# Hybrid trunk layer on one Trainium2 core: q and u of the input projection by seven half-block products per pair of feature blocks

## The reference

```python
h = rms_norm(x, mix_norm_g[l])
proj = h @ w_in[l]
u_a, v_a, q, k, v = jnp.split(proj, splits, axis=-1)      # 512, 512, 512, 128, 128 columns
y_a = spatial_gating(u_a, v_a, sgu_ln_g[l], sgu_ln_b[l], sgu_w[l], sgu_b[l])
y_b = window_sink_attention(q..., k..., v..., sinks[l], rel_bias)
y_a = rms_norm(y_a, group_norm_g[l, :D_A])
y_b = rms_norm(y_b, group_norm_g[l, D_A:])
x = x + jnp.concatenate([y_a, y_b], axis=-1) @ w_out[l]
h = rms_norm(x, ffn_norm_g[l])
x = x + (jax.nn.silu(h @ w_gate[l]) * (h @ w_up[l])) @ w_down[l]
return rms_norm(x, final_norm_g)
```

## Time and profile before

| what | value |
|---|---|
| median of 3 runs | 931.95 us (931.64 to 932.1) |
| span of the profiled execution | 930.2 us |
| TensorE busy | 921.3 us, 99% of the span |
| VectorE, ScalarE, GpSimd busy | 551.3, 403.6 and 329.1 us |
| mean granted TensorE clock | 0.998 |

### The profile page before, as it was taken

How to read it: one execution, slowest core, us unless ns; L and a number is a source line. 1 busy time by engine, 2 the same in 40 slices (tenths; PEclk the granted TensorE clock), 3 DMA queues, 4 the chain that set the end, 5 groups by cost and what they waited for, 6 DMA issues and landing times.

```text
span 930.2 us, 11930 instructions
## 1 busy us (share of the span) xinstructions
PE 921.3 (99%) x4277; PEld 757.5 (81%) x4277; DVE 551.3 (59%) x812; ACT 403.6 (43%) x833; POOL 329.1 (35%) x344
## 2 busy tenths in 40 slices
PE   9999999999999999999999999999999999999997
PEld 7888888878778878888888888888888888888885
DVE  5655773576677966564553645537446676544753
ACT  6743541465655733333333323333335355434451
POOL 1410000022125288575674765755753100000022
PEclk9999999999999999999999999999999999999999
DMA  9621312312224334726437365273557897656643
GB/s 337 229 79 57 89 41 88 88 46 87 73 98 130 102 114 158 226 77 218 153 108 227 99 195 179 90 241 90 182 179 259 317 394 230 188 198 194 191 138 133
DMA packets 132000, 147.02 MB, mean 158 GB/s; under 512 B 16281, under 2 KB 92645, under 8 KB 131941
## 3 DMA queue, kind: packets, MB, share of 16 engines
q1 hardware_dynamic: 131268, 145.86, 48.3%
q10 hardware_dynamic: 672, 0.40, 0.1%
HBM read 105.73 MB, written 40.50 MB: 157 GB/s over the span
## 4 chain that ended last, share of the span: by engine, by line
PE 94%; issue 2%; DVE 2%; DMA 1%; ACT 0%; POOL 0%; DVEq 0%; POOLq 0%; ACTq 0%
PE ps L703 30%; PE ps L705 29%; PE ps L704 29%; PE ps L830 1%; PE ps L849 1%; PE ps L907 1%; PE ps L840 1%; PE ps L779 1%; DMA A22s<-in_w_gate 1%; DVE P_lo L1703 0%; DMA small<-in_mix_gT 0%; DVE T_lo L1690 0%; PE ps L733 0%; PE ps L736 0%; PE ps L739 0%
## 5 line engine op out<-in xcount | busy, mean ns | idle before, releaser
L1703 DVE TENSOR_TENSOR P_lo<-P_raw,P_hi 128x512 fp32r<-128x512 f32 x132 | 118.1, 910 | 82.5 <-ACT P_hi L1227 75.2
L703 PE MATMUL ps<-T_hi,P_hi 128*128 128x512 f32 x352 | 137.1, 389 | 0.0
L705 PE MATMUL ps<-T_hi,P_lo 128*128 128x512 f32 x352 | 136.9, 389 | 0.0
L704 PE MATMUL ps<-T_lo,P_hi 128*128 128x512 f32 x352 | 136.9, 389 | 0.0
L703 PE MATMUL ps<-rb_hi,ra_hi 128*128 128x512 f32 x308 | 119.8, 389 | 0.0
L704 PE MATMUL ps<-rb_lo,ra_hi 128*128 128x512 f32 x308 | 119.8, 389 | 0.0
L705 PE MATMUL ps<-rb_hi,ra_lo 128*128 128x512 f32 x308 | 119.8, 389 | 0.0
L647 POOL TENSOR_TENSOR wd<-wd 128x256 f32<-128x256 f32 x88 | 82.9, 942 | 95.0 <-DMA wd<-in_w_down 89.9
L1328 ACT ACTIVATE ra_hi<-ra 128x512 fp32r<-128x512 f32 x77 | 48.6, 632 | 98.3 <-DMA rb<-w_down_T 58.1
L1783 DVE TENSOR_TENSOR ra_lo<-ra,ra_hi 128x512 fp32r<-128x512 f32 x77 | 56.2, 730 | 37.6 <-ACT ra_hi L1328 37.3
L1227 ACT ACTIVATE P_hi<-P_raw 128x512 fp32r<-128x512 f32 x132 | 76.6, 620 | 3.5 <-POOL P_raw L607 3.5
(11 more groups left out here) (208 smaller groups left out, 1911.4 us busy)
## 6 DMA issues: line engine op xcount, KB each, us to landing
wd<-in_w_down SPq DMA_DIRECT2D x44, 256.0 KB, 3.3
w_down_T<-wd SPq DMA_DIRECT2D x22, 512.0 KB, 5.0
ra<-act_S SPq DMA_DIRECT2D x44, 256.0 KB, 2.7
rb<-w_down_T SPq DMA_DIRECT2D x44, 256.0 KB, 3.0
act_S<-Q SPq DMA_DIRECT2D x33, 256.0 KB, 3.7
ra<-act_A SPq DMA_DIRECT2D x33, 256.0 KB, 5.0
rb<-in_w_down SPq DMA_DIRECT2D x33, 256.0 KB, 5.9
P_raw<-in_w_gate SPq DMA_DIRECT2D x22, 256.0 KB, 3.7
```

The source lines that it names most:

```text
L703: mm(dst, lhs[0], rhs[0], start=start, stop=False, skip_group_check=onto)
L704: mm(dst, lhs[0], rhs[1], start=False, stop=False, skip_group_check=onto)
L705: return mm(dst, lhs[1], rhs[0], start=False, stop=stop, skip_group_check=onto)
L1703: tt(w_l[p, m][:], src[:], w_h[p, m][:].bitcast(F32), ALU.subtract).then_inc(w_split, 1)
```

## The change

For each of four pairs of feature blocks (q0 with q1, q2 with q3, u0 with u1, u2 with u3) the product of a 1024 x 256 block of w_in with the two halves of the rows is seen as 2x2 blocks times 2x2 blocks, of 512 in k, and done by seven products of 12 (`in_product`) in place of eight of 12. The work goes stage by stage: P1 for the four pairs, then P2, P6, P5, P7, P3 and P4, in banks 0, 1, 2 and 7 for one family (accumulated) and 5 and 6 for the other.

- The combinations of x (D1 to D4) are built from a second load of xT: GpSimd subtracts, ScalarE scales by `mix_g` and makes the hi part, VectorE the lo part. The gain is now in hT, and no longer in the weights.
- The combinations of the weights (s1 = A21 + A22, s2 = s1 - A11, A11 - A21, A12 - s2) are GpSimd sums of freshly loaded blocks.
- Products are taken out by ScalarE (`product_copy`, 12), summed by VectorE (`product_add`, 12) and GpSimd (U + V, 4), and multiplied by `roots` on VectorE (`corner`, 16).
- The spatial blocks now all lie in P1 and P2, and the mixed values go back into `vn`. The gates and square sums go to GpSimd, the value copies to ScalarE. The woA blocks and the woB loads get new places. The totals of the first norm are taken in two halves, with a root each. The gelus of the last three blocks of u come behind the exponentials of row block 0.

```diff
-    ITEMS = ["k", "v", "u0", "u1", "u2", "u3", "A0", "A1", "A2", "q0", "A3", "q1", "q2", "q3"]
-    UNITS = [(c, h) for c in ("k", "v", "u0", "u1", "u2", "u3") for h in range(2)]
-    UNITS += [(f"q{t}", h) for h in range(2) for t in range(G)]
+    ITEMS = ["k", "v"]
+    UNITS = [(c, h) for c in ITEMS for h in range(2)]
+    IN_BANK_A, IN_BANK_B = (0, 1, 2, 7), (5, 6)
+    IN_ORDER = {p: (2, 3, 0, 1) if p == "P4" else (0, 1, 2, 3) for p in PR}
+    GATES = ((0, 1), (2, 1), (1, 0), (3, 0), (0, 0), (2, 0), (1, 1), (3, 1))
+    YA_SUMS = ((1, 0, 2), (2, 3, 4), (2, 0, 5), (2, 3, 6), (1, 0, 7), (1, 3, 8))
...
 GpSimd
+            for k in range(4):
+                pool.wait_ge(d_scaled, D_SCALED["D4"] + k + 1)
+                pool.wait_ge(combo_hi, k + 1)
+                combine(D_raw["D4"][:, k], D_raw["D4"][:, k], D_hi["D2"][:, k].bitcast(F32), ALU.subtract).then_inc(d_summed, 1)
+                pool.wait_ge(combo_ready, k + 1)
+                pool.wait_ge(d_summed, 12 + 2 * k + 1)
+                combine(D_raw["D4"][:, k], D_raw["D4"][:, k], D_lo["D2"][:, k].bitcast(F32), ALU.subtract).then_inc(d_summed, 1)
+            gate(0)
+            for i in range(4):
+                pool.wait_ge(slot_in[i], 4 * BLOCK[i])
+                combine(wA_raw[i][:], stg[i][:], wA_raw[i][:], ALU.subtract).then_inc(w_summed, 1)
+            gate(1)
+            for i in range(4):
+                pool.wait_ge(copied, copied_at("P5", i))
+                combine(U[:, i], U[:, i], V[:, i], ALU.add).then_inc(uv_added, 1)
+                pool.wait_ge(slot_in[4 + i], 2 * BLOCK[i])
+                combine(wB_raw[i][:], wB_raw[i][:], s2[i][:], ALU.subtract).then_inc(w_summed, 1)
+            ya_sum(0)
+            gate(2)
+            gate(3)
+            ya_sum(1)
+            gate(4)
+            ya_sum(2)
+            gate(5)
+            ya_sum(3)
+            gate(6)
+            gate(7)
+            rootA(0)
+            ya_sum(4)
+            ya_sum(5)
...
 TensorE
+            def in_product(p, i):
+                pe.wait_ge(w_split, in_split_at(p, i))
...
+                elif p == "P5":
+                    pe.wait_ge(combo_ready, 8)
+                    if i < 2:
+                        pe.wait_ge(c_summed, added_at("P2", i + 2))
+                    else:
+                        pe.wait_ge(copied, copied_at("P5", i - 2))
...
+                for k in range(4):
+                    last = split_mm(ps[:, in_bank(p, i), :], (hi[:, k], lo[:, k]), (rows[0][:, k], rows[1][:, k]), k == 0 and not onto, k == 3, onto)
+                last.then_inc(prod_done, 1)
...
             def value_windows(w):
-                if w in (0, 3):
+                if w < 2:
                     pe.wait_ge(ya_mixed, 2 * HA)
                 else:
-                    pe.wait_ge(ya_summed, 2 * HA - 2)
+                    pe.wait_ge(vwin_ready, w - 1)
...
-            unit(NQ1)
+            in_product("P3", 0)
+            value_windows(0)
+            value_windows(1)
+            in_product("P3", 1)
+            value_windows(2)
+            value_windows(3)
+            in_product("P3", 2)
             logits(0)
-            unit(NQ1 + 1)
-            unit(NQ1 + 2)
+            in_product("P3", 3)
+            for i in IN_ORDER["P4"][:3]:
+                in_product("P4", i)
             probs_T(0, 0)
-            unit(NQ1 + 3)
+            in_product("P4", IN_ORDER["P4"][3])
             probs_T(0, 1)
             logits(1)
             values(0)
+            ya_totals(0)
...
 ScalarE
+            for i in range(4):
+                in_weight_hi("P5", i)
+                d_scale("D3", i)
+                if i >= 2:
+                    u_gelu(i - 2)
+            for k in range(4):
+                d_scale("D4", k)
...
+            for i in range(4):
+                in_weight_hi("P7", i)
+                product_copy("P5", i)
+                d_to_hi("D4", i)
...
+            ya_hi_rows(0)
+            ya_hi_rows(1)
+            ya_square(0)
+            ya_square(1)
+            u_gelu(2)
+            woA_piece(2)
+            u_gelu(3)
+            woA_piece(3)
+            value_copy(0)
+            value_copy(1)
...
             for _half in probabilities(0):
                 pass
+            u_gelu(5)
+            u_gelu(6)
+            u_gelu(7)
+            ya_hi_rows(4)
+            ya_square(4)
+            ya_hi_rows(5)
+            ya_square(5)
             probs_to_sbuf(0, 0)
+            ya_hi_rows(6)
+            ya_square(6)
+            ya_hi_rows(7)
             probs_to_sbuf(0, 1)
+            ya_square(7)
...
 VectorE
+            for i in range(4):
+                in_weight_lo("P5", i)
+            for k in range(4):
+                d_to_lo("D3", k)
+            for i in range(4):
+                in_weight_lo("P7", i)
+                d_to_lo("D4", i)
+            in_weight_lo("P3", 0)
+            product_add("P7", 0)
+            corner("P7", 0)
+            in_weight_lo("P3", 1)
+            woA_piece(0)
+            product_add("P7", 1)
+            corner("P7", 1)
+            in_weight_lo("P3", 2)
+            woA_piece(1)
+            product_add("P7", 2)
+            corner("P7", 2)
+            in_weight_lo("P3", 3)
+            ya_lo_rows(0)
+            product_add("P7", 3)
+            corner("P7", 3)
```

More of the change, by code:

```diff
@@ L300, in hybrid_trunk_layer @@
         wd_in, wd_summed, wd_out = sem("wd_in"), sem("wd_summed"), sem("wd_out")
-        step_in = [sem(f"step_in{n}") for n in range(NSLOT)]
         y_in, step_hi, step_split, step_done, prod_out, y_added = (
@@ new lines, in product_add, with corner @@
+            def product_add(p, i):
+                dve.wait_ge(prod_done, in_at(p, i))
+                if p == "P2":
+                    dve.wait_ge(copied, copied_at("P1", i))
+                else:
+                    dve.wait_ge(uv_added, i + 1)
+                dst = {"P2": GP, "P7": V, "P3": U}[p]
+                tt(dst[:, i], ps[:, in_bank(p, i), :], dst[:, i], ALU.add).then_inc(c_summed, 1)
+            def corner(p, i):
+                f, half = CORNER[p]
+                if p == "P4":
+                    dve.wait_ge(prod_done, in_at(p, i))
+                    src = ps[:, in_bank(p, i), :]
+                else:
+                    dve.wait_ge(c_summed, added_at(p, i))
+                    src = {"P2": GP, "P7": V, "P3": U}[p][:, i]
+                if i < 2:
+                    if p == "P7" and i == 0:
+                        dve.wait_ge(ya_gated, 2)
+                    chunks = "p (c q) -> p c q"
+                    stt(qT[half][:, :, 2 * i + f, :], src.rearrange(chunks, q=CH), SCALE, roots[half][:].rearrange(chunks, q=CH), ALU.mult, ALU.mult).then_inc(c_out, 1)
+                else:
+                    tt(GATE_U[2 * CORNERS.index(p) + i - 2], src, roots[half][:], ALU.mult).then_inc(c_out, 1)
@@ new lines, in ya_lo_rows, with ya_total_sums @@
+            def ya_lo_rows(g):
+                h, half = GATES[g]
+                rows = slice(HT * half, HT * half + HT)
+                dve.wait_ge(ya_hi_ready, g + 1)
+                tt(ya[:, rows, 1, h, :], vn[:, h, rows], ya[:, rows, 0, h, :].bitcast(F32), ALU.subtract).then_inc(ya_ready, 1)
+            def ya_total_sums(half):
+                dve.wait_ge(ya_total, half + 1)
+                nc.vector.tensor_reduce(ssqA[:, HT * half:HT * half + HT], ps[:, 7, :].rearrange("p (t n) -> p t n", n=P), AX.X, ALU.add).then_inc(ssqA_ready, 1)
@@ L1579, in _ @@
-            evict(NQ0 + 3)
-            evict(NQ1)
+            for i in range(4):
+                in_weight_lo("P2", i)
+            ya_mix(0)
+            ya_mix(1)
+            d_to_lo("D2", 2)
+            d_to_lo("D2", 3)
+            in_weight_lo("P6", 0)
+            ya_mix(2)
+            ya_mix(3)
+            for i in range(4):
+                d_to_lo("D1", i)
+                if i:
+                    in_weight_lo("P6", i)
+                if i == 2:
+                    ya_mix(4)
+                    ya_mix(5)
+                product_add("P2", i)
+                corner("P2", i)
@@ new lines, in _ @@
+            in_weight_lo("P3", 2)
+            woA_piece(1)
+            product_add("P7", 2)
[4 more added lines that the diff above has]
+            corner("P7", 3)
+            woA_piece(2)
+            product_add("P3", 0)
+            corner("P3", 0)
+            ya_lo_rows(1)
+            woA_piece(3)
+            product_add("P3", 1)
+            corner("P3", 1)
+            in_weight_lo("P4", 0)
+            ya_lo_rows(2)
@@ L1582, in add_bias @@
+            product_add("P3", 2)
+            corner("P3", 2)
+            in_weight_lo("P4", 2)
             def add_bias(r):
```

659 lines of the change are left out of this document (423 added, 236 removed).

## The result

The changed kernel takes 943.54 us (median of 4 runs, 942.83 to 944.71) against 931.98 us for the kernel before on the same chip: ratio 1.0126, 95% interval 1.0112 to 1.014. The profiled execution has a span of 941.0 us against 930.2: +10.8. The prediction said +6.4 and 938.4 us, with P3(2) 11 us late and a lower clock in new gaps as a rival of its own. The measured time lies in its whole range (926 to 946 us) and above the range of the forecast's own case (934 to 942).

What follows compares the result with a forecast made beforehand. TensorE, 99% busy, bounds the kernel; GpSimd and VectorE together decide the change. Output projection 5.3 late, plus 0.7 and 0.4, gives +6.4 on the 930.2 us span: 936.6, measured 938.4; whole range 926 to 946, own case 934 to 942.

Steps and rivals of the forecast that it cites:

- P3(2): Third product of P3, input projection: can start at 153.5 us and not 142.4, 11.1 us late, spending the whole gain.
- the forecast's own case: Whole kernel: +6.4 us on the profiled span, 938.4 us measured, own range 934 to 942 us; chance 0.55.
- Removed work: Input projection on TensorE: 384 products become 336, 48 fewer at 0.2267 us each, 10.9 us less.
- P5(2): Third product of P5, due 118.8 us: 0.5 to 4 us late, waiting for ScalarE's copy of P5(0); swallowed by the later wait.
- Transfers, `mix_g`, the items at 0: Input projection: extra loads and issues, the gain moved from wv to xT, and merged k and v operations each cost 0.
- Exclusion: GpSimd additions and VectorE operations with two SBUF inputs run one at a time: 1.74 us a pair, 44.5 us from 105.5.
- Corner(P7,3): VectorE's last corner of P7, needed by the next chain: 150.0 us by the exclusive sum, taken as 150.3 with waits.
- The clock at 0: TensorE's granted clock: the forecast's sum has no term for a fall in the new gaps, so 0 us.
- rival 3: Granted clock falls to half speed in new gaps before P3(2) and in the tail: 943.8 to 946.5 us; chance 0.12.
- The tail: From P3(2) to the output projection: 26.7 us through ScalarE's queue, 5.9 over TensorE's own 20.8; output projection at 180.2.
- the one microsecond of exclusion: Between P3(2) and the output projection: one microsecond of the GpSimd and VectorE lock, raising 25.7 us to 26.7.
- The rival on the other side: GpSimd and VectorE slip into each other's gaps, without the lock: P3(2) starts at 142.9, 926.8 us; chance 0.21.

## Why the prediction was right, and where it wasn't

**Removed work: right.** Up to 118.4 us every product stands within 0.3 us of where the calendar without waits has it, at 0.227 us pitch. The last of the 24 matmuls of P5(0) and (1) starts at 118.40, so the next was possible at 118.6, and P5(2) was due at 118.8.

**Transfers, `mix_g`, the items at 0: right.** No wait of TensorE in the stage is released by a transfer. The one that mattered showed up only in experiments: the woB loads, which I had costed at 0 because `out_unit(0,2)` isn't late. They held ScalarE in front of row block 1's exponentials, 2.8 us, once all ahead of them was faster.

**Exclusion: right, and by the estimate above the largest cost, but the length of GpSimd's own work stands right behind it.** The pair is 1.69 to 1.72 us against 1.74 in the sum. The Trainium skill (SBUF — State Buffer, section "SBUF: two separate sides") has an exclusive lock on the shared port pair, and for a VectorE operation with two SBUF inputs it limits it to GpSimd operations that read SBUF. This case's runs agree: additions hold VectorE's splits to 1.76 us, memsets of nearly the same length, which read nothing, leave them at 0.69, and sums from PSUM stay at 0.68. Corner(P7,3) ended at 150.5 against 150.3. So close a hit is luck in part. The sum assumed both engines without idle time; the trace has VectorE idle for 4.27 us before 122.55 and GpSimd for 3.73 us before 145.50, and in return VectorE works alone for much of 142 to 150.

**P5(2): 4.4 us late against 0.5 to 4, and swallowed by the later wait but for 1 us at most:** shown by the run with P5's copies first. The prediction expected TensorE's longest idle time before value windows 2 and 3; it lies before P5(2), 4.36 against 4.23 us.

**P3(2): 154.41 against 153.5.** The value windows start at 152.79, where I had 153.1. From there to P3(2) are 1.62 us where I had 0.44. The clock is 0.8 of that: the eight transposes of windows 0 and 1, at full clock, take 0.80 us from start to next start (144.78 to 145.58). The other 0.4 is a price that I had too low.

**The clock at 0: the term that failed.** The forecast's sum has nothing for it; rival 3 had it, at 943.8 to 946.5 us, and it came true beside the forecast, just below that range. On TensorE's path behind the waits the trace has, from start to next start and against the same work at full clock, 0.8 us for the transposes, 0.7 for three products of P3(2), 0.9 for the values (1.90 against 1.01), 0.4 for the totals and 1.5 for the first eight products of the output projection (3.44 against 1.95 in the kernel before): 4.3 us. With the 6.4 of the forecast that is 10.7 against 10.8 measured. The account by TensorE's rows alone says too much, though: the run with transposes took 2.8 us of the 4.3 away, had 1.2 more at P3(2), and gained about 1, because the softmax of row block 1 stood next.

**The tail: right but for the clock.** From P3(2) to the output projection it took 28.8 us against 26.7, of which 2.0 by the rows above is clock. Of the one microsecond of exclusion that the forecast counted there, 0.6 is seen: a split of P4's weights ahead of the maxima takes 1.32 us beside a gate (161.75), and the first exponential comes 6.45 us after the start of `logits(0)` (157.99 to 164.44) where the sum without exclusion had 5.7. The output projection was 8.3 us late against 5.3, and behind it 2.5 were lost against 1.1, of which 1.5 is clock.

**The rival on the other side was sized wrongly.** I gave 926.8 us without exclusion, with the corner at 143.9 as the point from which the kernel is faster. The run with long memsets has no exclusion and its corner at 141.7, and takes 934.4. Its tail from P3(2) is 29 us and not 25.7, since TensorE, arriving 8 us earlier, waits 6.3 us for ScalarE's copies behind the gates. A memset tile lasts longer there (1.49 us) than an addition alone (1.25), so this run is harder than the rival's condition; by the estimate above the change as written, without exclusion, would be about level with the kernel before and not 5 us faster. I had worked the tail out as one chain from P3(2); it hangs on the gates and on the softmax.

**What stays open:** how the cost of exclusion divides between lost VectorE time, lost GpSimd time and the clock in the gaps; what additions without exclusion would really take; and what remains of the cost of GpSimd's pace if its gates alone are sped up.

## What to carry to other kernels

Fewer products on a full TensorE are a gain only if the engines that make the operands have room in the order in which they are wanted. Add up the exclusive time of GpSimd and VectorE as one queue first, and then check whether VectorE alone can hold it: moving twenty sums away from GpSimd gave 7.0 of 11.6 us, and only the order in the queues, mended wait by wait, gave the rest. The longest wait in a profile can cost almost nothing: that of 4.4 us, with 2.5 us of slow products behind it, cost at most 1. Ask of each what waits next, and don't add up what edits of order gave alone: the three here were worth 1.0, 0 and 3.1 us alone, and 2.0 together on top of the moved sums. When an edit leaves the time where a rival had it, look at what the wait now hangs on: twice the rival's number came for another reason, the load of woB.

## What the runs showed of the hardware that was not expected

A wait of TensorE can cost more than its length. After 4.36 us of idle time twelve products took 5.26 us instead of 2.72, while after 1.74 us, in the run with twenty sums on VectorE, the next product ran at full speed:

```profile
120.39 0.47 PE L851 MATMUL ps<-D_hi,wB_hi 128*128 128x512 f32 x1 [1.74 <-ACT V L1340]
```

The length of one wait doesn't decide it in these rows. Behind a wait of 2.0 us before `probs_T(0,1)` four transposes took 1.01 us in the kernel after (176.19) and 0.63 in the run with twenty sums on VectorE (171.12).

GpSimd memsets run beside VectorE's splits without a loss that the rows show: 0.05 us for 128x16 and 0.095 for 128x64, and splits at 0.68 to 0.69 meanwhile.
